# Other order and banks for the turned input norm and second norm, the last block of the down product in halves, and the arena's stationary tiles moved onto the weights' grid of 4096 bytes

## The chip, the cores and the metric

The kernel runs on one core of one Trainium2 chip. The metric is the device time of one execution in microseconds (us), lower is better. Engines: PE (TensorE), ACT (ScalarE), DVE (VectorE), POOL (GpSimd) and SP (SyncE, which here only issues the DMAs of the weights).

## What is computed

Two transformer blocks on 256 tokens of width 2048, all in float32. Cut to what matters here:

```python
def first_block(x, mem, ...):
    mem_h = rms_norm(mem, mem_norm_g)
    x = x + hybrid_mixer(rms_norm(x, mix_norm_g), w_in, ...)            # pooling and gated delta net
    x = x + memory_cross_attention(rms_norm(x, xa_norm_g), mem_h, w_xq, w_xkv, w_xo)
    x = x + conv_glu_ffn(rms_norm(x, ffn_norm_g), w_gate, w_up, ..., w_down)
    return rms_norm(x, final_norm_g)

def second_block(x, c, w_ada, b_ada, pre_norm_mix, ...):
    mod = silu(c) @ w_ada + b_ada
    shift_m, scale_m, gate_m, shift_f, scale_f, gate_f = split(mod, 6)
    h = rms_norm(x, pre_norm_mix) * (1 + scale_m) + shift_m
    o = concat(nsa_mixer(h @ w_in ...), moba_mixer(h @ w_in ...)) @ w_o
    x = x + gate_m * rms_norm(o, post_norm_mix)
    h = rms_norm(x, pre_norm_ffn) * (1 + scale_f) + shift_f
    f = square(relu(h @ w_up)) @ w_down
    return x + gate_f * rms_norm(f, post_norm_ffn)
```

## The kernel before, in words

**Products.** Every large product runs through `product` (PE), `phase`/`split_hi` (ACT) and `phase`/`split_lo` (DVE), one phase after another in the order of `plan()`: `wi0` to `wi4` (the first `w_in`), `mix_out`, `xkva`, `xkvb`, `xq`, `xo`, `ffn1a`, `down1a`, `ffn1b`, `down1b`, `w_in2a` to `w_in2c`, `w_oa`, `w_ob`, and four times `up2`, `down2`. A weight unit is 512 rows by 512 columns (428 in `wi`, 432 in `w_in2a`), a DMA by SP into one of four `raw` buffers. ACT rounds it to a high part `whi` (line 1295), DVE subtracts for the low part `wlo` (line 1715), in two halves each; the ring holds four halves, that is two units. SP, ACT and DVE are ahead of PE by at most these buffers: ACT waits for a half to be read (`mm_done`) before it overwrites it, SP for a unit to be split (`unit_used`). The first two units of a phase are split at the end of the phase ahead (`LEAD`).

Per unit PE makes 8 triples: high by high (line 869), low weights by high (870), high weights by low (871). The activations are the stationary operand (128 x 128; its load is the PEld row of the same line), the weights the moving one (up to 512 columns). The stationary tiles are turned (features on the partitions), split into a high and a low part too: `hhi`, `hlo` in fixed memory for most phases; in the arena, which is laid out anew for every stage, `mhi`, `mlo` (phases `xkva`, `xkvb`), `bhi`, `blo` (`ffn1a`, `ffn1b`), `flo` (`down1a`, `down1b`, whose high part `fhi` lies over `hhi` and `hlo`) and `f2hi`, `f2lo` (the four `down2`). In memory the ring begins at `ring0`, `hhi` 49152 bytes per partition further, the arena (`arena0`) 101920 bytes further. 24 of the iterations also carry the side product (`ada`): four more units per iteration, which DVE alone multiplies and adds (lines 1701 and 1703) for `mod`.

**A norm before a product.** The raw input is turned by PE (line 845, four transposes of 128 x 128 per group of two feature tiles, into one half of a two-bank tile), ACT takes the upper part out of the bank times the gain, DVE the lower part; the scale of the row is applied when the product is evacuated. For the input this is `raw_turn(0, k)`, `raw_upper(0, k)` (line 1356) and `raw_lower(0, k)` (line 1770) with k from 0 to 7, all in the two halves of `TA`; turn n waits for `norm_lo` n - 1. Turns 0 to 3 stand ahead of phase `wi0`, 4 and 5 after its first unit, 6 and 7 after its second. ACT and DVE take all eight before the third unit is split, and then compute `csig` (a sigmoid) on ACT and DVE.

**The second block's first norm** follows `down1b`. Its last addition to `x` (line 1784, 128 x 1024) and the product with the final gain (`final_gain`, line 2050) run on DVE after the first two units of `w_in2a` are split; ACT takes the squares (line 1587), DVE the mean, ACT the root (line 1596, for which it loads a table), DVE the reciprocal. `xn_f` is the scaled input: its first quarter by DVE (line 2066), the others by ACT (`pre2_scaled`, line 1601). `pre2_turn(g)` turns it into four banks, `pre2_full(g)` (DVE, line 2075) applies gain and shift, `hhi` is ACT's copy of that (line 1609), and `pre2_lower(g)` (DVE, line 2082) the rest. Groups 0 to 3 are turned ahead of `w_in2a`, 4 and 5 after its first unit, 6 and 7 after its second. DVE does all eight full and low parts before it goes on to the phase, where the first unit in its order is one of the side product, and the third weight unit comes after it.

## Time and profile before

| | |
|---|---|
| median of 3 runs | 3002.54 us (3001.13 to 3006.74) |
| profiled execution: its time, its span | 3002.88 us, 3001.1 us |
| mean granted PE clock | 0.971 |
| PE, PEld busy | 2847.8 us (95%), 2396.0 us (80%) |
| DVE, ACT, POOL busy | 1797.8 us (60%), 1309.7 us (44%), 182.4 us (6%) |
| HBM read | 575.66 MB, 193 GB/s over the span |
| chain that ended last | PE 90%, DVE 6%, ACT 2% |

Busy time of PE is modelled, since matmuls overlap: a matmul's duration is longer than the distance to the next one's start, and only gaps and distances between starts tell the pace. In a group of the profile, the numbers are count, busy time, mean ns of one, idle time of the engine before. In a timeline: start, duration, engine, line, operation, output and inputs, shape, how many were merged, and in brackets how long the engine had stood idle and what ended that. PEclk is the granted clock, 1.00 for the upper level (2.4 GHz) and 0.50 for the lower (1.2 GHz).

### The profile page before, as it was taken

What the parts mean: (1) busy time and instruction counts of PE and PEld (TensorE: products, weight loads), DVE (VectorE), ACT (ScalarE), POOL (GpSimd) and SP (SyncE); (2) the same over time, 40 slices, a digit from 0 to 9 for tenths busy, and PEclk for the clock granted to TensorE, in tenths of its full rate; (3) what the DMA queues carried; (4) which work ended last, traced back from release to release, by engine and by line L of the source; (5) the groups of instructions that cost most, each with busy time, mean ns of one, the idle gap of its engine ahead of it and who ended that gap; (6) DMA issues with size and microseconds to landing.
All of it is one profiled execution on the core that took longest, in us unless ns stands there. A gap on an engine that the chain in (4) does not pass through costs nothing.

```text
span 3001.1 us, 35854 instructions
## 1 busy us (share of the span) xinstructions
PE 2847.8 (95%) x13510; PEld 2396.0 (80%) x13510; DVE 1797.8 (60%) x2008; ACT 1309.7 (44%) x1620; POOL 182.4 (6%) x135
## 2 busy tenths in 40 slices
PE   8998989999899999999999889987879999999997
PEld 7998968888788888788888689776768787888885
DVE  4476567776466555665555477954675655744454
ACT  5454234454435445434444444324444444344442
POOL 0000520000000000000000004610000000000000
PEclk9999999999999999999999899978989999999998
DMA  7453038887556555675555388650455765755552
GB/s 261 155 170 110 1 142 278 272 269 259 181 197 224 182 182 182 228 246 179 174 187 199 124 302 298 226 182 15 157 179 176 245 227 207 267 192 186 183 184 96
DMA packets 292399, 579.57 MB, mean 193 GB/s; under 512 B 9072, under 2 KB 46096, under 8 KB 290992
## 3 DMA queue, kind: packets, MB, share of 16 engines
q1 hardware_dynamic: 290720, 565.03, 55.9%
q0 software_dynamic: 1552, 12.76, 1.1%
q8 instruction: 89, 1.46, 0.2%
q14 instruction: 38, 0.31, 0.0%
HBM read 575.66 MB, written 2.10 MB: 193 GB/s over the span
## 4 chain that ended last, share of the span: by engine, by line
PE 90%; DVE 6%; ACT 2%; issue 1%; DMA 0%; POOL 0%; DVEq 0%; SPq 0%; ACTq 0%
PE GP L869 27%; PE GP L870 26%; PE GP L871 26%; PE TA L845 2%; PE TB L468 2%; DVE ada_acc L1703 1%; PE TB L845 1%; DVE wlo L1715 1%; PE TA L1222 1%; PE GP L454 1%; PE TB L886 0%; DVE o L2148 0%; DVE x L2149 0%; ACT whi L1295 0%; DVE small L545 0%
## 5 line engine op out<-in xcount | busy, mean ns | idle before, releaser
L1715 DVE TENSOR_TENSOR wlo<-raw,whi 128x1024 fp32r<-128x1024 f32 (+2 forms) x904 | 1088.9, 1220 | 809.4 <-ACT whi L1295 799.2
L1295 ACT CAST whi<-raw 128x1024 fp32r<-128x1024 f32 (+2 forms) x904 | 921.3, 1029 | 1206.4 <-PE GP L871 1160.4
L869 PE MATMUL GP<-whi,hhi 128*128 128x512 f32 (+2 forms) x1792 | 695.8, 388 | 33.5 <-DVE wlo L1715 27.4
L870 PE MATMUL GP<-wlo,hhi 128*128 128x512 f32 (+2 forms) x1792 | 686.2, 383 | 0.0
L871 PE MATMUL GP<-whi,hlo 128*128 128x512 f32 (+2 forms) x1792 | 685.9, 383 | 0.0
L869 PEld LDWEIGHTS GP<-whi,hhi 128*128 128x128 f32 x1792 | 342.0, 191 | 88.7 <-issue 27.4
L871 PEld LDWEIGHTS GP<-whi,hlo 128*128 128x128 f32 x1792 | 341.4, 191 | 53.0
L870 PEld LDWEIGHTS GP<-wlo,hhi 128*128 128x128 f32 x1792 | 342.0, 191 | 51.8 <-issue 1.0
L1703 DVE SCALAR_TENSOR_TENSOR ada_acc<-raw,csig,ada_acc 128x512 f32<-128x512 f32 x360 | 284.4, 790 | 10.2
L869 PE MATMUL GP<-whi,bhi 128*128 128x512 f32 x704 | 280.4, 398 | 0.0
L870 PE MATMUL GP<-wlo,bhi 128*128 128x512 f32 x704 | 278.3, 395 | 0.0
L871 PE MATMUL GP<-whi,blo 128*128 128x512 f32 x704 | 278.2, 395 | 0.0
L869 PE MATMUL GP<-whi,f2hi 128*128 128x512 f32 x512 | 204.7, 400 | 4.7 <-DVE wlo L1715 4.7
L871 PE MATMUL GP<-whi,f2lo 128*128 128x512 f32 x512 | 202.5, 395 | 0.0
L870 PE MATMUL GP<-wlo,f2hi 128*128 128x512 f32 x512 | 202.4, 395 | 0.0
L871 PEld LDWEIGHTS GP<-whi,blo 128*128 128x128 f32 x704 | 132.3, 188 | 32.1
L870 PEld LDWEIGHTS GP<-wlo,bhi 128*128 128x128 f32 x704 | 132.3, 188 | 30.8
L869 PEld LDWEIGHTS GP<-whi,bhi 128*128 128x128 f32 x704 | 132.3, 188 | 30.8
L869 PE MATMUL GP<-whi,fhi 128*128 128x512 f32 x352 | 139.3, 396 | 2.5 <-DVE wlo L1715 2.5
L870 PE MATMUL GP<-wlo,fhi 128*128 128x512 f32 x352 | 140.7, 400 | 0.0
L871 PE MATMUL GP<-whi,flo 128*128 128x512 f32 x352 | 137.0, 389 | 0.0
L869 PEld LDWEIGHTS GP<-whi,f2hi 128*128 128x128 f32 x512 | 96.2, 188 | 29.1 <-issue 6.5
(394 smaller groups left out, 2688.2 us busy)
## 6 DMA issues: line engine op xcount, KB each, us to landing
raw<-in_w_up SPq DMA_DIRECT2D x108, 1024.0 KB, 5.4
raw<-in_w_down SPq DMA_DIRECT2D x108, 1024.0 KB, 5.0
raw<-in_w_ada SPq DMA_DIRECT2D x96, 1024.0 KB, 5.1
raw<-in_w_gate SPq DMA_DIRECT2D x44, 1024.0 KB, 5.1
raw<-in_w_in SPq DMA_DIRECT2D x48, 856.0 KB, 4.7
raw<-in_w_xkv SPq DMA_DIRECT2D x32, 1024.0 KB, 5.5
raw<-in_w_in SPq DMA_DIRECT2D x24, 1024.0 KB, 5.0
raw<-in_w_in SPq DMA_DIRECT2D x24, 864.0 KB, 5.0
```

Source lines behind the costliest of these rows:

```text
L454: m = pe.matmul(o[:, h * T:h * T + u["L"]], l, r, start=(d == 0), stop=(d == n - 1), skip_group_check=True)
L468: m = pe.matmul(bank[:, j * P:j * P + P], l, r, start=(d == 0), stop=(d == len(terms) - 1), skip_group_check=True)
L845: return pe.transpose(dst, src, ident[0:n, 0:n] if n != P else ident)
L869: pe.matmul(o, ahi[:, kt, t], whi[r][:, k, 0:q.width], start=first, stop=False)
L870: pe.matmul(o, ahi[:, kt, t], wlo[r][:, k, 0:q.width], start=False, stop=False)
L871: m = pe.matmul(o, alo[:, kt, t], whi[r][:, k, 0:q.width], start=False, stop=last)
L1222: m = pe.matmul(TA[:, 512:543], w1c[:, l, :], rc1[:, l, :], start=(l == 0), stop=(l == 31))
L1295: nc.scalar.copy(whi[(2 * g + s) % NRING][:, :, 0:q.width], raw[j % NSLOT][:, 2 * s:2 * s + 2, 0:q.width])\
L1703: m = nc.vector.scalar_tensor_tensor(ada_acc[:, :], raw[j % NSLOT][:, k, :], c, ada_acc[:, :], ALU.mult, ALU.add)
L1715: TTo(wlo[r][:, :, 0:q.width], raw[j % NSLOT][:, 2 * s:2 * s + 2, 0:q.width], whi[r][:, :, 0:q.width].bitcast(F32), ALU.subtract).then_inc ...
```

## The change

Four things:

1. `level()` rounds an arena address up to the next one with the remainder that `ring0` has by 4096. It is applied ahead of `mhi`/`mlo`, of `bhi`/`blo` (and so `flo` and the tiles behind them) and of `f2hi`/`f2lo`: each moves up by 480 bytes.
2. The input's norm: turns 2 and 3, 6 and 7 go to `TB`; turns 4 to 7 follow `wi0`'s first unit; ACT and DVE take banks 6 and 7 after the third unit's split; the squares come one unit later, the sigmoid for `csig` four units later, and DVE's product for it behind `wi4`.
3. The last block of `down1b` is added and multiplied by the final gain row half by row half (`last_block`), ACT squares each half as it comes, and a square root of a constant ahead of the squares loads the root's table.
4. The second norm: six groups are turned ahead of `w_in2a`, into six banks (`GP` 2 and the second half of `TB` are new), 6 and 7 after its first unit; DVE goes two full parts, two low parts; groups 6 and 7 come after the third unit's split on ACT and DVE.

```diff
--- before.py
+++ after.py
+        def level(at):
+            return at + (ring0 - at) % 4096
...
-        ar = Arena(); ar.at = arena0 + 4 * NH * 2 * D
+        ar = Arena(); ar.at = level(arena0 + 4 * NH * 2 * D)
         mhi = ar("mhi", [P, KT, T], F32R); mlo = ar("mlo", [P, KT, T], F32R)
...
-        ar = Arena()
+        ar = Arena(); ar.at = level(arena0)
         bhi = ar("bhi", [P, KT, T], F32R); blo = ar("blo", [P, KT, T], F32R)
         fhi = nc.alloc_sbuf_tensor_at("fhi", [P, 24, T], F32R, offset=hh0); flo = ar("flo", [P, 24, T], F32R)
...
         o3 = ar("o3", [P, NH, D])
+        ar.at = level(ar.at)
         f2hi = ar("f2hi", [P, 16, T], F32R); f2lo = ar("f2lo", [P, 16, T], F32R)
...
-        pre2_bank = [TA[:, 0:512], TA[:, 512:1024], TB[:, 0:512], GP[:, 3, :]]
-
-        def raw_bank(n):
-            return TA[:, 512 * (n % 2):512 * (n % 2) + 512]
+        pre2_bank = [TA[:, 0:512], TA[:, 512:1024], TB[:, 0:512], GP[:, 3, :], GP[:, 2, :], TB[:, 512:1024], TA[:, 0:512], TA[:, 512:1024]]
+
+        def raw_bank(n, s=None):
+            t = TB if s == 0 and n % 4 >= 2 else TA
+            return t[:, 512 * (n % 2):512 * (n % 2) + 512]
...
-                if n >= 2:
+                if s == 0:
+                    if k >= 4:
+                        pe.wait_ge(S("norm_lo"), k - 3)
+                else:
                     pe.wait_ge(S("norm_lo"), n - 1)
...
-                    points={(0, 0, u): lambda u=u: (raw_turn(0, 2 * u + 4), raw_turn(0, 2 * u + 5)) for u in range(2)})
+                    points={(0, 0, 0): lambda: [raw_turn(0, k) for k in range(4, 8)]})
...
             def pre2_turn(g):
-                pe.wait_ge(*((S("p2_x"), g // 2) if g >= 2 else (S("p2_x0"), 1)))
+                pe.wait_ge(*((S("p2_x"), g // 2) if g >= 2 else (S("p2_x0"), 4)))
                 if g == 3:
                     pe.wait_ge(S("evac1"), 1 + PH["down1b"].ev1)
-                if g >= 4:
-                    pe.wait_ge(S("norm_f"), g - 3)
+                if g == 5:
+                    pe.wait_ge(S("ada_read"), PH["w_in2a"].ada0 + 1)
+                if g >= 6:
+                    pe.wait_ge(S("norm_lo"), 32 + g - 5)
                 for j in range(2):
                     for h in range(NH):
-                        m = turn(pre2_bank[g % 4][:, j * T + h * P:j * T + h * P + P], xn_f[:, h, (2 * g + j) * P:(2 * g + j + 1) * P])
+                        m = turn(pre2_bank[g][:, j * T + h * P:j * T + h * P + P], xn_f[:, h, (2 * g + j) * P:(2 * g + j + 1) * P])
                 m.then_inc(S("norm_t"), 1)
 
-            for g in range(4):
+            for g in range(6):
                 pre2_turn(g)
             product(PH["w_in2a"], hhi, hlo, lambda u: (S("norm_lo"), 32 + 2 * u + 2), first=lambda: None,
-                    points={(0, 0, u): lambda u=u: (pre2_turn(2 * u + 4), pre2_turn(2 * u + 5)) for u in range(2)})
+                    points={(0, 0, 0): lambda: (pre2_turn(6), pre2_turn(7))})
...
             split_hi(order[0], 0, 1)
-            for k in range(4, 8):
-                raw_upper(0, k)
-            nc.scalar.activation(csig[:, :], cvec[:, :], ACT.Sigmoid).then_inc(S("csig"), 1)
+            raw_upper(0, 4)
+            raw_upper(0, 5)
...
-                  head={3: [lambda it: raw_square(0, (0,))], 4: [lambda it: raw_square(0, (1,))], 5: [lambda it: raw_root(0)]})
+                  head={3: [lambda it: (raw_upper(0, 6), raw_upper(0, 7))], 4: [lambda it: raw_square(0, (0,))], 5: [lambda it: (raw_square(0, (1,)), raw_root(0))],
+                        7: [lambda it: nc.scalar.activation(csig[:, :], cvec[:, :], ACT.Sigmoid).then_inc(S("csig"), 1)]})
...
-                act.wait_ge(*((S("fin_g"), b + 1) if i else (S(f"evac{b % 2}"), 2 + PH["down1b"].ev0 + b // 2)))
+                if b < 3:
+                    act.wait_ge(*((S("fin_g"), b + 1) if i else (S(f"evac{b % 2}"), 2 + PH["down1b"].ev0 + b // 2)))
                 for h in range(NH):
+                    if b == 3:
+                        act.wait_ge(*((S("p2_x0"), h + 2) if i else (S("evac1"), 1 + PH["down1b"].ev1) if h else (S("p2_x0"), 1)))
...
+            nc.scalar.activation(froot[:, 0:1], C("ones", 0, 1), ACT.Sqrt)
             final_squares(3, 0)
             final_squares(3, 1)
...
-            pre2_scaled(1)
-            for g in range(8):
-                if g in (2, 4):
-                    pre2_scaled(g // 2 + 1)
+            def pre2_upper(g):
                 act.wait_ge(S("norm_f"), g + 1)
                 nc.scalar.copy(hhi[:, 2 * g:2 * g + 2, :], fbx[g % 2].rearrange("p (a b) -> p a b", b=T)).then_inc(S("norm_hi"), 1)
-            phase(PH["w_in2a"], store(PH["w_in2a"], p2, lastcol=NSA_W - W2A), head={5: [lambda it: act.wait_ge(S("fin_x"), 2)]})
+
+            pre2_scaled(1)
+            pre2_scaled(2)
+            for g in range(6):
+                if g == 4:
+                    pre2_scaled(3)
+                pre2_upper(g)
+            phase(PH["w_in2a"], store(PH["w_in2a"], p2, lastcol=NSA_W - W2A), head={3: [lambda it: (pre2_upper(6), pre2_upper(7))],
+                                                                                         5: [lambda it: act.wait_ge(S("fin_x"), 2)]})
...
-            phase(PH["wi0"], {}, head={4: [lambda it: raw_mean(0)], 5: [lambda it: raw_scale(0)]})
+            phase(PH["wi0"], {}, head={3: [lambda it: (raw_lower(0, 6), raw_lower(0, 7))], 5: [lambda it: (raw_mean(0), raw_scale(0))]})
             for k in range(1, 5):
                 phase(PH[f"wi{k}"], slots(todo, f"wi{k}"), ahead=(k < 4))
+            dve.wait_ge(S("csig"), 1)
+            link(TTo(csig[:, :], csig[:, :], cvec[:, :], ALU.mult))
             dve.wait_ge(S("cst_in"), 16)
...
+            def last_block(it):
+                dve.wait_ge(S("mm_done"), block_end(PH["down1b"], it, 3) + NRING)
+                c = slice(1536, 2048)
+                TTo(x[:, 0, c], GP[:, 2, :], x[:, 0, c], ALU.add).then_inc(S("p2_x0"), 1)
+                TTo(x[:, 1, c], GP[:, 3, :], x[:, 1, c], ALU.add).then_inc(S("evac1"), 1)
+                dve.wait_ge(S("p2_x0"), 1)
+                TTo(xg[:, 0, c], x[:, 0, c], fgb[:, c], ALU.mult).then_inc(S("p2_x0"), 1)
+                dve.wait_ge(S("evac1"), 1 + PH["down1b"].ev1)
+                TTo(xg[:, 1, c], x[:, 1, c], fgb[:, c], ALU.mult).then_inc(S("p2_x0"), 1)
+
+            for b in range(3):
                 hooks[5 * b + 7] = hooks[5 * b + 7] + [lambda it, b=b: final_gain(b)]
+            hooks[22] = [last_block]
...
-            pre2_full(0)
-            for g in range(1, 8):
+            def pre2_pair(g):
                 pre2_full(g)
-                pre2_lower(g - 1)
-            pre2_lower(7)
+                pre2_full(g + 1)
+                pre2_lower(g)
+                pre2_lower(g + 1)
+
+            for g in (0, 2, 4):
+                pre2_pair(g)
 
             def final_x(h):
                 nc.vector.tensor_scalar(x[:, h, :], xg[:, h, :], frs[:, h:h + 1], None, ALU.mult).then_inc(S("fin_x"), 1)
 
-            phase(PH["w_in2a"], {}, head={3: [lambda it: final_x(0)], 4: [lambda it: final_x(1)]})
+            phase(PH["w_in2a"], {}, head={3: [lambda it: pre2_pair(6)], 4: [lambda it: final_x(0)], 5: [lambda it: final_x(1)]})
```

The instructions on ACT at the start. Names: `whi0` to `whi3` are the ring's high halves, `raw2` holds the third unit. Before:

```order
L1295 CAST whi2_51<-raw1 128x2x428
L1295 CAST whi3_52<-raw1 128x2x428
L1356 ACTIVATE hhi<-TA,tab 128x256 x8
L1410 ACT_TABLE_LOAD
L1410 ACTIVATE csig<-tab 128x16
L1295 CAST whi0_49<-raw2 128x2x428
```

and with the change:

```order
L1307 CAST whi2_51<-raw1 128x2x428
L1307 CAST whi3_52<-raw1 128x2x428
L1368 ACTIVATE hhi<-TA,tab 128x256 x4
L1307 CAST whi0_49<-raw2 128x2x428
L1307 CAST whi1_50<-raw2 128x2x428
L1368 ACTIVATE hhi<-TB,tab 128x256 x4
```

The third unit moved ahead of two of the four banks, the table load and the sigmoid.

DVE in the second norm, from group 5's full part (two instructions per group at line 2075 before, 2107 now) to the third unit. Before:

```order
L2075 TENSOR_SCALAR flat<-TA,tab,shifts 128x256 x2
L2082 TENSOR_TENSOR hlo<-flat,hhi 128x512
L2075 TENSOR_SCALAR flat<-TB,tab,shifts 128x256 x2
L2082 TENSOR_TENSOR hlo<-flat,hhi 128x512
L2075 TENSOR_SCALAR flat<-GP,tab,shifts 128x256 x2
L2082 TENSOR_TENSOR hlo<-flat,hhi 128x512 x2
L1701 TENSOR_SCALAR ada_acc<-raw2,csig 128x512
L1703 SCALAR_TENSOR_TENSOR ada_acc<-raw2,csig,ada_acc 128x512 x3
L1715 TENSOR_TENSOR wlo0_53<-raw3,whi0_49 128x2x432
```

and with the change:

```order
L2107 TENSOR_SCALAR flat<-TB,tab,shifts 128x256 x2
L2114 TENSOR_TENSOR hlo<-flat,hhi 128x512 x2
L1722 TENSOR_SCALAR ada_acc<-raw2,csig 128x512
L1724 SCALAR_TENSOR_TENSOR ada_acc<-raw2,csig,ada_acc 128x512 x3
L1736 TENSOR_TENSOR wlo0_53<-raw3,whi0_49 128x2x432
L1736 TENSOR_TENSOR wlo1_54<-raw3,whi1_50 128x2x432
L2107 TENSOR_SCALAR flat<-TA,tab,shifts 128x256 x4
L2114 TENSOR_TENSOR hlo<-flat,hhi 128x512 x2
```

The side product's unit and the third unit now stand ahead of groups 6 and 7.

## Rows read from the trace of the kernel before

**Rows 1.** The page of the kernel before, part 1: busy time of each engine.

```profile
PE 2847.8 (95%) x13510; PEld 2396.0 (80%) x13510; DVE 1797.8 (60%) x2008; ACT 1309.7 (44%) x1620; POOL 182.4 (6%) x135
```

**Rows 2.** Groups of instructions by shape, PE: count, busy us, mean ns of one.

```profile
L870 PE MATMUL GP<-wlo,hhi 128*128 128x512 f32 x1216 | 477.1, 392 | 0.0
L870 PE MATMUL GP<-wlo,bhi 128*128 128x512 f32 x704 | 278.3, 395 | 0.0
L870 PE MATMUL GP<-wlo,f2hi 128*128 128x512 f32 x512 | 202.4, 395 | 0.0
L870 PE MATMUL GP<-wlo,fhi 128*128 128x512 f32 x352 | 140.7, 400 | 0.0
L871 PE MATMUL GP<-whi,flo 128*128 128x512 f32 x352 | 137.0, 389 | 0.0
L870 PE MATMUL GP<-wlo,mhi 128*128 128x512 f32 x256 | 101.2, 395 | 0.0
```

**Rows 3.** Timeline of PE in `w_oa`, `hhi` stationary: the 1st and 18th `L870`.

```profile
2150.25 0.39 PE L870 MATMUL GP<-wlo,hhi 128*128 128x512 f32 x1
...
2161.81 0.39 PE L870 MATMUL GP<-wlo,hhi 128*128 128x512 f32 x1
```

**Rows 4.** Timeline of PE in `ffn1a`, `bhi` stationary: the 1st and 17th `L870`.

```profile
1000.27 0.40 PE L870 MATMUL GP<-wlo,bhi 128*128 128x512 f32 x1
...
1011.47 0.40 PE L870 MATMUL GP<-wlo,bhi 128*128 128x512 f32 x1
```

**Rows 5.** Timeline of PE in `down1a`, `fhi` stationary: the 1st and 18th `L870`.

```profile
1310.04 0.40 PE L870 MATMUL GP<-wlo,fhi 128*128 128x512 f32 x1
...
1321.94 0.40 PE L870 MATMUL GP<-wlo,fhi 128*128 128x512 f32 x1
```

**Rows 6.** Timeline just after a sum of the side product: 1st and 4th `L870`.

```profile
1841.23 0.39 PE L870 MATMUL GP<-wlo,hhi 128*128 128x512 f32 x1
...
1843.31 0.39 PE L870 MATMUL GP<-wlo,hhi 128*128 128x512 f32 x1
```

**Rows 7.** Timeline of the start: ACT, DVE, PE; idle before in brackets.

```profile
24.74 1.57 ACT L1356 ACTIVATE hhi<-TA,tab 128x256 fp32r<-128x256 f32 x4 [4.02 <-PE TA L845]
...
28.73 2.01 DVE L1715 TENSOR_TENSOR wlo<-raw,whi 128x856 fp32r<-128x856 f32 x2 [0.69 <-ACT whi L1295]
...
29.93 0.70 PE L869 MATMUL GP<-whi,hhi 128*128 128x428 f32 x1 [4.79 <-DVE wlo L1715]
```

**Rows 8.** Windows: busy of PE, PEld, DVE, ACT, POOL, then PEclk, DMA share, GB/s.

```profile
30.00:35.00 5.00, 5.00 (x19) 4.72 (x20) 2.86 (x4) 5.00 (x7) 0.00 (x0) 0.70 0.57 179
```

**Rows 9.** The same view around the second norm.

```profile
1733.00:1736.00 3.00, 2.84 (x8) 2.66 (x9) 3.00 (x4) 0.00 (x0) 0.00 (x0) 0.50 0.80 302
1736.00:1744.00 8.00, 8.00 (x42) 7.54 (x40) 6.21 (x9) 1.74 (x2) 0.00 (x0) 0.98 1.01 387
```

**Rows 10.** Timeline of the second norm, all engines.

```profile
1697.36 1.22 DVE L1784 TENSOR_TENSOR x<-GP,x 128x1024 f32<-128x1024 f32 x1
...
1701.68 1.28 ACT L1596 ACT_TABLE_LOAD   x1
...
1704.36 1.97 PE L845 MATMUL TA<-cst,xn_f 128*128 128x128 f32 x8 [8.95 <-DVE xn_f L2066]
...
1709.81 0.70 PE L869 MATMUL GP<-whi,hhi 128*128 128x432 f32 x1 [1.78 <-issue]
...
1719.63 0.46 PE L869 MATMUL GP<-whi,hhi 128*128 128x432 f32 x1 [1.26 <-DVE hlo L2082]
...
1729.08 0.48 DVE L1701 TENSOR_SCALAR ada_acc<-raw,csig 128x512 f32<-128x512 f32 x1
...
1731.95 2.03 DVE L1715 TENSOR_TENSOR wlo<-raw,whi 128x864 fp32r<-128x864 f32 x2
...
1733.16 0.70 PE L869 MATMUL GP<-whi,hhi 128*128 128x432 f32 x1 [7.67 <-DVE wlo L1715]
...
1741.99 1.74 ACT L1295 CAST whi<-raw 128x864 fp32r<-128x864 f32 x2 [10.30 <-DMA raw<-in_w_in]
```

More of the change, by code:

```diff
@@ L162, in program @@
         hh0 = (nc.sbuf_base + 31) // 32 * 32
+        assert (hh0 - ring0) % 4096 == 0
         hhi = fixed("hhi", [P, KT, T], F32R)
@@ L926, in raw_turn @@
                     for h in range(NH):
-                        m = turn(raw_bank(n)[:, j * T + h * P:j * T + h * P + P], X[:, h, (2 * k + j) * P:(2 * k + j + 1) * P])
+                        m = turn(raw_bank(n, s)[:, j * T + h * P:j * T + h * P + P], X[:, h, (2 * k + j) * P:(2 * k + j + 1) * P])
                 m.then_inc(S("norm_t"), 1)
@@ L1355, in raw_upper @@
                 for j in range(2):
-                    m = nc.scalar.activation(hi[:, 2 * k + j, :], raw_bank(n)[:, j * T:j * T + T], ACT.Copy, scale=gains[:, g_, 2 * k + j:2 * k + j + 1])
+                    m = nc.scalar.activation(hi[:, 2 * k + j, :], raw_bank(n, s)[:, j * T:j * T + T], ACT.Copy, scale=gains[:, g_, 2 * k + j:2 * k + j + 1])
                 m.then_inc(S("norm_hi"), 1)
@@ L1769, in raw_lower @@
                 for j in range(2):
-                    m = nc.vector.scalar_tensor_tensor(lo[:, 2 * k + j, :], raw_bank(n)[:, j * T:j * T + T], gains[:, g_, 2 * k + j:2 * k + j + 1],
+                    m = nc.vector.scalar_tensor_tensor(lo[:, 2 * k + j, :], raw_bank(n, s)[:, j * T:j * T + T], gains[:, g_, 2 * k + j:2 * k + j + 1],
                                                        hi[:, 2 * k + j, :].bitcast(F32), ALU.mult, ALU.subtract)
@@ L1835, in _ @@
             split_lo(order[0], 0, 1)
-            for k in range(4, 8):
-                raw_lower(0, k)
-            dve.wait_ge(S("csig"), 1)
-            link(TTo(csig[:, :], csig[:, :], cvec[:, :], ALU.mult))
+            raw_lower(0, 4)
+            raw_lower(0, 5)
             def gate_first():
@@ L2052, in _ @@
             hooks = add_to_x(PH["down1b"])
-            for b in range(4):
+            def last_block(it):
[8 more added lines that the diff above has]
+            for b in range(3):
                 hooks[5 * b + 7] = hooks[5 * b + 7] + [lambda it, b=b: final_gain(b)]
+            hooks[22] = [last_block]
             hooks[4] = [lambda it: modulation(0, 0, 4)]
@@ L2074, in pre2_full @@
                     kt = 2 * g + j
-                    m = nc.vector.tensor_scalar(fbx[g % 2][:, j * T:j * T + T], pre2_bank[g % 4][:, j * T:j * T + T], gains[:, 4, kt:kt + 1],
+                    m = nc.vector.tensor_scalar(fbx[g % 2][:, j * T:j * T + T], pre2_bank[g][:, j * T:j * T + T], gains[:, 4, kt:kt + 1],
                                                 shifts[:, 0, kt:kt + 1], ALU.mult, ALU.add)
```

## The prediction

> **What bounds the kernel now.** I read the page first: PE is busy 95% of the span and no other engine over 60% [rows 1]. So only two kinds of change can move the time: one in the pace at which PE takes its matmuls, and one in the gaps in which PE stands still. The sum is made against the profiled execution (3002.88 us, with 1.8 us outside its span of 3001.1); the median of the runs is 3002.54, 0.3 us under it.
>
> For the pace I took the groups by shape. All large products are the same triple (`L869`, `L870`, `L871`), 512 columns wide, with different stationary tiles. With `hhi`/`hlo` as stationaries a matmul takes 392 ns in the mean, with the arena's `bhi`, `f2hi` and `mhi` 395, and where `fhi` and `flo` are mixed, 400 and 389 [rows 2]. These are latencies, and what counts is the distance between starts. In the timeline, 17 triples on `hhi` take 2161.81 - 2150.25 = 11.56 us, 680 ns each [rows 3]; 16 on `bhi`/`blo` take 11.20 us, 700 ns each [rows 4]; 17 on `fhi`/`flo` take 11.90 us, again 700 [rows 5]. It isn't the work beside them: `w_oa` and `down1a` both run with the side product, `ffn1a` runs without it. What the slower ones share is that a stationary lies in the arena.
>
> For the gaps I took the timelines of the two places that the change rearranges. At the start, PE stands 4.79 us before the third weight unit: DVE makes its low half at 28.73, after the norm's last two banks, whose upper parts ACT takes from 24.74 on [rows 7]. After the gap the granted clock falls to its lower level (1.2 GHz): the 5 us window has 0.70, that is 3.0 us at 0.50 [rows 8]. At the second norm, PE stands 8.95, 1.78, 1.26 and 7.67 us [rows 10], and again the clock is 0.50 after the last gap [rows 9].
>
> **The change, part 1: the arena's stationaries.** `ring0` to `arena0` is 101920 bytes by the tiles' shapes, 24 x 4096 + 3616. Every arena tile of a product so lies 3616 past the weights' grid of 4096, `hhi` and `hlo` lie 0 past it (49152 = 12 x 4096), and the change puts the former to 0 too, by 480 bytes. It adds no instruction. Triples with an arena stationary: `ffn1a` and `ffn1b` 384 + 320 = 704, the four `down2` 512, `down1a` and `down1b` 192 + 160 = 352, `xkva` and `xkvb` 256, as the counts in [rows 2] say; 1824 in all. If they go from 700 to 680 ns: 1824 x 20 ns = 36.5 us. Not all of it, since `hhi` triples don't always run at 680: after an interruption of the stream (turns, or the sum of the side product) the first three take 2.08 us, 693 ns each [rows 6]. Some 54 such interruptions lie in the arena's phases (22 gate and up turns, 8 + 4 single ones, 10 sums, 10 starts); 54 x 3 x 13 ns = 2.1 us. I take **34 us**. The bounds are 0 (place doesn't matter) and 36.5. For a loss see the rivals.
>
> All of it lies on PE's path: ACT and DVE wait for PE in these phases, not the other way, as 60% and 44% of busy time allow [rows 1]. What could be late next is the weights' transfer. With the side product, 8 + 4 units of 1.05 MB go with 64 triples: 12.6 MB in 64 x 0.68 + 1 = 44.5 us, 283 GB/s, under the 387 that one window shows [rows 9]. DVE then has 16 x 1.24 + 4 x 3.1 = 32 us of work in 44.5. Neither becomes the bound.
>
> The row speaks against a rule here. By the Trainium skill, page "TensorE: Matmul & The Clock Gate", Part 2, step 1, loading the next stationary takes no SBUF bandwidth from the running matmul, and by its section on the back-to-back gap 512 columns are 216 ns apart whatever the tiles. By that, part 1 would be worth 0 and all triples would take 647 ns; the trace disagrees with both (680 and 700).
>
> **Part 2: the start.** Turns 0 to 3 go to four banks (two of `TA`, two of `TB`), 4 to 7 all follow the first unit, and on ACT and DVE the third unit's split stands ahead of banks 6 and 7. Step by step: turns 4 and 5 end at about 19.3 as before, 6 and 7 at 20.4 (the input's last columns must have landed; POOL, which waits for them all, went on at 18.4, a bound of a microsecond on this). The second unit then runs 20.4 to 25.0. ACT takes banks 4 and 5 until 20.7 and the third unit until 22.5, DVE its low half until 23.7: before 25.0, so PE goes on. Banks 6 and 7 follow on ACT until 24.1 and on DVE until 25.5, due at 29.7 for the fourth unit. The gap of 4.79 us goes, and with it 3.0 us at half clock, in which PE did the work of 1.6: 1.4 us more. **6.2 us**, between 4 and 6.5. The squares and the root come one unit later and are due only at the first evacuation; the sigmoid with its table load (1.28 us, as [rows 10] show one) moves behind that evacuation, where ACT waits for PE. `csig`'s product now stands on DVE ahead of the delta net, 0.2 us, covered by the turn that DVE waits for there.
>
> **Part 3: the second norm.** From PE's last matmul of `down1b` (1704.36 - 8.95 = 1695.41) to the fifth unit of `w_in2a` (its split starts at 1741.99, its first matmul 2.2 us later, 1744.2) it is now 48.8 us. In order:
> - *The wait.* The last block's addition (1.22 us) is halved, so ACT's four squares start some 0.55 us earlier, and the square root's table load (1.28 us) is over before them. The root waited for the load's end, about 0.5 us after the mean was there. 8.95 becomes about 7.95.
> - *The turns.* Eight transposes take 1.97 us at half clock [rows 10]; six groups of four so take 5.2. DVE's order (two full, two low) has the second low part about 4.4 us after the first turn starts, so PE doesn't wait the 1.78 us any more. Before: 3.7 + 1.8 = 5.5.
> - *The first unit.* 1709.81 to 1717.14, 7.3 us, most of it at half clock. Same work after about the same idle time; I take 7.3 again, between 5 and 8.6 (24 matmuls at 0.36).
> - *Second unit.* Two groups, then no wait for a low part: 1.0 + 4.7. Before 2.5 + 4.6 with the 1.26 us.
> - *Turns and the long wait.* 1.2 + 7.67 us go. DVE has the low part of group 5 some 10.9 us after the first turn, then the side product's unit (from 1729.08 to the split at 1731.95: 2.9), then the third unit's (2.0): 15.9 us after the first turn, when PE is 5.2 + 7.3 + 1.0 + 4.7 = 18.2 past it. Covered by 2.3 us.
> - *Third and fourth unit.* 9.4 at full clock, before 11.05, since the stretch after the gap ran at 0.50.
>
> Sum: 7.95 + 5.2 + 7.3 + 5.7 + 9.4 = 35.6 against 48.8: **13.2 us**, between 8 and 15. What is queued behind the moved work: the scaling of `x` (2 x 1.28 us) now follows the pair 6, 7 on DVE, and the fifth unit's low half ends up about 0.6 us ahead of PE. That is the tightest spot. Raw units: the fifth is asked for when the side product's unit is free, now about 14 us earlier; before, it came late (ACT waited 10.3 us until 1741.99) as POOL's loads for the compression ran at the same time. These now start behind it, since POOL still waits for the last low part.
>
> **Sum.** 34 + 6.2 + 13.2 = 53.4; 3002.9 - 53.4 = 2949.5, against the median 2949. Anything within 0.2% (6 us) would be no change that can be told.
>
> **Rivals.**
> - *A. The place is not the reason.* Another thing that all arena tiles share sets the pace (that they lie above `hhi`, say), and the triples stay at 700. For it: no tile of a product lies low and off the grid, so the trace can't tell the two apart. Against it: the loads of `flo` and `fhi`, which differ in both, also differ in time (400 and 389). Then only parts 2 and 3 count: 3002.9 - 19.4 = 2983.5. The rule of the Trainium skill's page "TensorE: Matmul & The Clock Gate" cited above gives this time too.
> - *B. The norms' new order makes new waits.* Full parts in pairs hold ACT up, and the fifth unit comes late or the sixth (ACT waits for both scalings of `x`): half of part 3 and some of part 2 go, 2949 + 9 = 2958; the placement is untouched.
> - *C. Slower.* In the one place where loads on and off the grid alternate, the matmul under `flo`'s load takes 400 ns. If sharing the weights' remainder makes tiles this high collide, every arena matmul takes 400 instead of 395: 3 x 1824 x 5 ns = 27 us lost, less 19.4 gained: 3010.8. It decides from 3.5 ns a matmul on. Against it: `hhi` shares the remainder and has the shortest distance.
>
> **How the numbers follow.** The forecast has 0.75 (its own range 2942 to 2957), A 0.13, B 0.07, C 0.03, 0.02 for the rest near no change. The time is the forecast's, 2949. The range must take in B and reach to A: 2941 to 2985. Chances: faster 0.95 (forecast, A, B), same 0.02, slower 0.03.
>
> **What would show it.** Right: `L870` on `bhi`, `f2hi`, `mhi` at 392 or less in the groups and 680 ns between starts in `ffn1a`; no wait of PE for `wlo` within the first 60 us and a clock of 1.00 from 20 to 40; at the second norm one wait of about 8 us and none of over 1 us before the third unit. Part 1 is wrong if the distance stays 700. Part 3 is wrong if PE waits for `wlo` or `hlo` between the first turn and the sixth unit. If the sum is far under 53 with all three steps as said, a later phase has become bound by DVE or the transfers, and ACT would show long waits for `raw`.

## The result, and the profile after

| | before | after |
|---|---|---|
| median of four runs | 3002.26 us | 2951.80 us |
| range of the runs | 3001.13 to 3006.74 | 2948.91 to 2956.72 |
| profiled execution, its span | 3002.88, 3001.1 | 2952.63, 2950.9 |
| PE busy | 2847.8 us | 2812.7 us |

The ratio is 0.9831, with a 95% interval from 0.9814 to 0.9848: 50.5 us less. The forecast was 2949.0, with a range from 2941 to 2985.

The page of the changed kernel, busy time and granted clock, against [rows 1]:

```profile
PE 2812.7 (95%) x13510; PEld 2393.9 (81%) x13510; DVE 1794.3 (61%) x2010; ACT 1308.7 (44%) x1620; POOL 183.5 (6%) x135
...
PEclk9998999999999999999999999978989999999998
```

PE has the same number of instructions and 35 us less of busy time, and the rest of the 50 us went from its idle time. By shape, the groups that answer to [rows 2] (columns: line, engine, tiles, shape, count, busy us, mean ns of one, idle before):

```profile
L877 PE MATMUL GP<-wlo,hhi 128*128 128x512 f32 x1216 | 476.8, 392 | 0.0
...
L877 PE MATMUL GP<-wlo,bhi 128*128 128x512 f32 x704 | 273.9, 389 | 0.0
...
L877 PE MATMUL GP<-wlo,f2hi 128*128 128x512 f32 x512 | 199.8, 390 | 0.0
...
L877 PE MATMUL GP<-wlo,fhi 128*128 128x512 f32 x352 | 137.7, 391 | 0.0
L878 PE MATMUL GP<-whi,flo 128*128 128x512 f32 x352 | 137.6, 391 | 0.0
L877 PE MATMUL GP<-wlo,mhi 128*128 128x512 f32 x256 | 99.7, 389 | 0.0
```

With `bhi`, `f2hi` and `mhi` a matmul fell by 5 to 6 ns, the pair of 400 and 389 became 391 twice, and `hhi` stayed at 392. In the timeline of `ffn1a`, 16 triples now take 10.89 us, 681 ns each, where [rows 4] had 11.20:

```profile
934.52 0.40 PE L877 MATMUL GP<-wlo,bhi 128*128 128x512 f32 x1
...
945.41 0.39 PE L877 MATMUL GP<-wlo,bhi 128*128 128x512 f32 x1
```

The start, timeline of ACT, DVE and PE, which answers to [rows 7]:

```profile
18.92 1.04 PE L852 MATMUL TB<-cst,x 128*128 128x128 f32 x8
...
19.72 0.44 PE L876 MATMUL GP<-whi,hhi 128*128 128x428 f32 x1
...
20.13 1.73 ACT L1307 CAST whi<-raw 128x856 fp32r<-128x856 f32 x2
21.14 2.00 DVE L1736 TENSOR_TENSOR wlo<-raw,whi 128x856 fp32r<-128x856 f32 x2
21.73 1.59 ACT L1368 ACTIVATE hhi<-TB,tab 128x256 fp32r<-128x256 f32 x4
```

The third unit's low half (`L1736`) is made at 21.1, not at 28.7, ahead of the last two banks. The 4.79 us gap is gone, and with it the lower clock: the window that had 0.70 in [rows 8] has 1.00 (columns: window, its length, busy PE, PEld, DVE, ACT, POOL with counts, clock, DMA share, GB/s).

```profile
25.00:30.00 5.00, 5.00 (x28) 4.83 (x27) 2.74 (x3) 3.91 (x5) 0.00 (x0) 1.00 1.04 372
30.00:35.00 5.00, 5.00 (x27) 4.84 (x26) 1.82 (x4) 4.97 (x7) 0.00 (x0) 1.00 0.79 254
```

The second norm, PE's timeline, against [rows 10]. The turns follow one another, the first unit begins right behind them, and the waits of 1.78, 1.26 and 7.67 us are gone. What is left is one wait of 8.06 and, in the stretch shown, two small ones on `wlo`:

```profile
1676.13 1.97 PE L852 MATMUL TA<-cst,xn_f 128*128 128x128 f32 x8 [8.06 <-DVE xn_f L2098]
...
1680.80 0.44 PE L876 MATMUL GP<-whi,hhi 128*128 128x432 f32 x1
...
1685.59 1.03 PE L852 MATMUL TA<-cst,xn_f 128*128 128x128 f32 x8
1686.38 0.44 PE L876 MATMUL GP<-whi,hhi 128*128 128x432 f32 x1
...
1696.29 0.43 PE L876 MATMUL GP<-whi,hhi 128*128 128x432 f32 x1 [0.26 <-DVE wlo L1736]
...
1702.56 0.43 PE L876 MATMUL GP<-whi,hhi 128*128 128x432 f32 x1 [1.34 <-DVE wlo L1736]
```

To see where the 50.2 us of the span came from I laid the two traces side by side by the products' phases, each from its first matmul to its last:

| stretch | before | after | less |
|---|---|---|---|
| first four units of `wi0` | 28.96 | 21.85 | 7.1 |
| `mhi` (`xkva`, `xkvb`) | 185.18 | 180.58 | 4.6 |
| `bhi` (`ffn1a`, `ffn1b`) | 279.05 + 231.64 | 271.92 + 225.68 | 13.1 |
| `fhi` (`down1a`, `down1b`) | 138.65 + 112.62 | 136.65 + 109.50 | 5.1 |
| `f2hi` (four `down2`) | 93.72 + 93.72 + 90.23 + 94.06 | 91.41 + 93.01 + 87.71 + 91.84 | 7.8 |
| last matmul of `down1b` to last of `w_in2a` | 144.89 | 131.05 | 13.8 |
| everything else | | | -1.3 |

The first row is part 2 of the change, the sixth parts 3 and 4 (the prediction takes them together as its part 3), the four between them part 1 (30.6 us). The negative rest is mostly in `mix_out`, a product that the change leaves alone: it took 1.15 us longer, because the granted clock was lower for more of it (see below).

### The profile page after: what moved, and what is told of

It reads as the page before. It is cut to its first block, busy times and chain, and to the rows that moved or that the text cites. A ratio compares the mean times of both kernels' runs of the same rounds, so it can differ in the third digit from the quotient of the medians.

```text
span 2950.9 us, 35855 instructions
## 1 busy us (share of the span) xinstructions
PE 2812.7 (95%) x13510; PEld 2393.9 (81%) x13510; DVE 1794.3 (61%) x2010; ACT 1308.7 (44%) x1620; POOL 183.5 (6%) x135
## 4 chain that ended last, share of the span: by engine, by line
PE 90%; DVE 6%; ACT 2%; issue 1%; DMA 1%; POOL 0%; DVEq 0%; SPq 0%; ACTq 0%
PE GP L876 26%; PE GP L878 26%; PE GP L877 26%; PE TA L852 2%; PE TB L474 2%; DVE ada_acc L1724 1%; PE TB L852 1%; DVE wlo L1736 1%; PE TA L1234 1%; PE GP L460 1%; PE TB L893 1%; ACT whi L1307 0%; DVE o L2183 0%; DVE x L2184 0%; DVE small L551 0%
## 5 line engine op out<-in xcount | busy, mean ns | idle before, releaser
L1736 DVE TENSOR_TENSOR wlo<-raw,whi 128x1024 fp32r<-128x1024 f32 (+2 forms) x904 | 1086.2, 1219 | 779.5 <-ACT whi L1307 769.1
```

The costliest lines, as they stand in the source:

```text
L1736: TTo(wlo[r][:, :, 0:q.width], raw[j % NSLOT][:, 2 * s:2 * s + 2, 0:q.width], whi[r][:, :, 0:q.width].bitcast(F32), ALU.subtract).then_inc ...
```

## The experiments

Twelve kernels ran. They ask three things: whether place and order act apart from each other, what about the place matters, and which piece of each new order carries its gain. In short diffs, `-` is the changed kernel and `+` the experiment, unless said otherwise.

### Each half of the change alone: `e1_place`, `e2_norms`

`e1_place`, against the kernel before:

```diff
+        def level(at):
+            return at + (ring0 - at) % 4096
...
-        ar = Arena(); ar.at = arena0 + 4 * NH * 2 * D
+        ar = Arena(); ar.at = level(arena0 + 4 * NH * 2 * D)
...
-        ar = Arena()
+        ar = Arena(); ar.at = level(arena0)
         bhi = ar("bhi", [P, KT, T], F32R); blo = ar("blo", [P, KT, T], F32R)
...
+        ar.at = level(ar.at)
         f2hi = ar("f2hi", [P, 16, T], F32R); f2lo = ar("f2lo", [P, 16, T], F32R)
```

> The kernel before with the arena's stationaries at the weights' remainder and nothing else. Placement theory (part 1 as predicted): triples of mhi, bhi, fhi/flo and f2hi go from about 700 to about 681 ns, 34 us less, 2968 us. Interruption theory (rival A: the difference in before came from what ran beside those products, not from the address): triples stay at 700 ns, 3002 us. What the trace of the change suggests in between: the triples fall, but a little of it is given back in half-clock stretches, about 31 us less, 2971.

Measured: 2972.12 us, ratio 0.9897 [0.9882, 0.9912], 30.4 us less. The groups of its trace:

```profile
L874 PE MATMUL GP<-wlo,bhi 128*128 128x512 f32 x704 | 273.9, 389 | 0.0
...
L874 PE MATMUL GP<-wlo,f2hi 128*128 128x512 f32 x512 | 200.0, 391 | 0.0
```

They are those of the changed kernel to 1 ns, so the interruption theory falls. Most of the 3.6 us between 34 and 30.4 is a matter of the clock, shown below.

`e2_norms`, against the changed kernel:

```diff
         def level(at):
-            return at + (ring0 - at) % 4096
+            return at
```

> The change without its placement: only the order and the banks of the two norms, and the halves of the last block. If the two parts are independent, parts 2 and 3 as predicted give 19.4 us less than before, 2983 us; by the trace of the change (7.2 and 13.8 us) 21 less, 2981. If the norms' gain needed the faster products (its weights arriving in time), it would be under 12 us, over 2990.

Measured: 2982.81 us, ratio 0.9936 [0.9922, 0.9949], 19.7 us less than before. Its arena triples stay at 700 ns, and its `f2hi` phases are as long as before to 0.01 us each. The two halves add up within what the intervals allow (some 4 us on each): 30.4 + 19.7 = 50.1, and the whole change gave 50.5. The norms' order doesn't lean on the faster products.

### What about the address: `e3_grid`, `e4_low`, `e5_grid2`, `e12_grid3`

All arena tiles of a product lay off the weights' grid before and lie on it now, so the change alone can't say which grid it is. One kernel can hold several remainders, since each tile has its own phases. `e3_grid`:

```diff
-        ar = Arena(); ar.at = level(arena0 + 4 * NH * 2 * D)
+        ar = Arena(); ar.at = level(arena0 + 4 * NH * 2 * D) + 64
...
-        ar = Arena(); ar.at = level(arena0)
+        ar = Arena(); ar.at = level(arena0) + 256
...
-        fhi = nc.alloc_sbuf_tensor_at("fhi", [P, 24, T], F32R, offset=hh0); flo = ar("flo", [P, 24, T], F32R)
+        fhi = nc.alloc_sbuf_tensor_at("fhi", [P, 24, T], F32R, offset=hh0); ar.at += 256; flo = ar("flo", [P, 24, T], F32R)
...
-        ar.at = level(ar.at)
+        ar.at = level(ar.at) + 1024
```

> The change with four different remainders against the weights: mhi and mlo 64 bytes on, bhi and blo 256, flo 512, f2hi and f2lo 1024. Theory 64 (a stationary is slow only where its address is not a multiple of 64 bytes): every triple stays at 681 ns, 2952 us. Theory 4096 (it must lie at the weights' own remainder, as the change puts it): all four kinds go back to 700 ns, some 34 us more, 2985. A border in between (128, 512 or 1024) shows as some kinds fast and some slow.

Measured: 2955.69 us, ratio 0.9843 [0.9825, 0.9861]. `bhi` and `blo` now lie 256 bytes past the grid, `flo` 512 (256 and 256 more), `f2hi` and `f2lo` 1024. Only `mhi`, 64 bytes past it, is slow again; 256, 512 and 1024 are as good as 0:

```profile
L877 PE MATMUL GP<-wlo,bhi 128*128 128x512 f32 x704 | 273.9, 389 | 0.0
L877 PE MATMUL GP<-wlo,f2hi 128*128 128x512 f32 x512 | 199.8, 390 | 0.0
L878 PE MATMUL GP<-whi,flo 128*128 128x512 f32 x352 | 137.7, 391 | 0.0
...
L877 PE MATMUL GP<-wlo,mhi 128*128 128x512 f32 x256 | 101.2, 395 | 0.0
```

Neither theory holds as it was put: 64 isn't enough, and 4096 isn't needed.

`e4_low`, a pad of 32 bytes ahead of `hhi`:

```diff
+        fixed("shim", [P, 8])
         hh0 = (nc.sbuf_base + 31) // 32 * 32
-        assert (hh0 - ring0) % 4096 == 0
```

> The change with a pad of 32 bytes ahead of hhi, so that hhi, hlo and fhi, which lay at the weights' remainder in both kernels, lie 32 bytes off it; the arena's stationaries stay on it. Address theory: the triples of hhi (1216) and of fhi (352) go to 700 ns, 1568 x 19 ns = 30 us more, 2982. Region theory (the lower part of the memory is fast, the arena fast for another reason): hhi's stay at 681 ns, 2952 us.

Measured: 2979.33 us, ratio 0.9922 [0.9904, 0.994], 27.5 over the change. Low tiles and arena have changed places:

```profile
L877 PE MATMUL GP<-wlo,hhi 128*128 128x512 f32 x1216 | 484.1, 398 | 0.0
...
L877 PE MATMUL GP<-wlo,bhi 128*128 128x512 f32 x704 | 274.0, 389 | 0.0
```

`hhi`'s triples are 700 ns apart (1150 of them in the timeline), `bhi`'s 681. So the region is not the reason, the address is. One group did not follow: the triples of `wi0` to `wi4`, 428 columns wide, lose nothing here, 32 bytes off the grid. `wi4` (64 triples) takes 39.57 us from its first matmul to its last, and 39.81 in the change, with the same stationary tiles.

`e5_grid2` has other remainders in the same four places (`mhi` 128, `bhi` 64, `flo` 128, `f2hi` 384), `e12_grid3` three more (`mhi` 96, `bhi`, `blo` and `flo` 160, `f2hi` 224).

> The change with other remainders against the weights: mhi and mlo 128 bytes on, bhi and blo 64, flo 128, f2hi and f2lo 384. In the run before this one 64 was slow (mhi) and 256, 512 and 1024 fast. Theory 128: mhi, fhi/flo and f2hi at 681 ns, bhi (704 triples) at 700, 13 us more than the change, 2965. Theory 256: mhi, fhi/flo, f2hi and bhi all at 700 ns, 34 us more, 2985. If only mhi was slow there for a reason of its own, bhi stays at 681 too and mhi does not.

> The change with mhi and mlo 96 bytes off the weights' remainder, bhi, blo and flo 160, f2hi and f2lo 224. Period theory (a stationary is fast only where its distance from the weights is a multiple of 256 bytes, as 0, 256, 512 and 1024 were and 32, 64, 128, 192 and 384 were not): all three at 700 ns, 34 us over the change, 2985. If it is a matter of nearness or of certain remainders, one of them is at 681 or below.

Measured: `e5_grid2` 2979.75 us, ratio 0.9926 [0.9904, 0.9949]; `e12_grid3` 2984.32, ratio 0.9941 [0.9922, 0.9959]. The groups of `e5_grid2`:

```profile
L877 PE MATMUL GP<-wlo,bhi 128*128 128x512 f32 x704 | 277.4, 394 | 0.0
...
L877 PE MATMUL GP<-wlo,f2hi 128*128 128x512 f32 x512 | 202.0, 395 | 0.0
...
L877 PE MATMUL GP<-wlo,mhi 128*128 128x512 f32 x256 | 101.0, 395 | 0.0
```

All are slow: 128 is no grid either, and 384 is 128 past a multiple of 256. So `bhi` (160), `f2hi` (224) and `mhi` (96) in `e12_grid3`:

```profile
L877 PE MATMUL GP<-wlo,bhi 128*128 128x512 f32 x704 | 277.6, 394 | 0.0
L877 PE MATMUL GP<-wlo,f2hi 128*128 128x512 f32 x512 | 202.2, 395 | 0.0
...
L877 PE MATMUL GP<-wlo,mhi 128*128 128x512 f32 x256 | 101.5, 396 | 0.0
```

### Absolute or against the weights: `e6_all64`, `e7_ring64`, `e8_all128`

A pad ahead of the ring moves weights and stationaries together (`[P, 16]` is 64 bytes, `[P, 32]` in `e8_all128` 128):

```diff
+        fixed("shim", [P, 16])
         ring0 = (nc.sbuf_base + 31) // 32 * 32
```

`e7_ring64` has the same pad and a second one, also of 64 bytes, ahead of `hh0`, and `level` counts from `hh0`. The stationaries are back on multiples of 128 bytes, the weights alone lie 64 off them, and every stationary lies 64 bytes past the weights' remainder.

> The change with a pad of 64 bytes ahead of the weights' ring: weights and all stationaries still have one and the same remainder, but each address lies 64 bytes off a multiple of 128. Relative theory (stationaries and weights must agree, the words of the change): all triples 681 ns, 2952 us. Absolute theory (a stationary must lie on a multiple of 128 bytes): all 3040 triples of 512 columns at 700 ns, 58 us more, 3010.

> The change with the weights' ring alone 64 bytes off a multiple of 128, stationaries all on one. Relative theory: all triples 700 ns, 3010 us. Absolute theory for the stationary alone: 681 ns, 2952 us. If the moving side has the same rule, the triples are slower than 681, by an amount that no row shows yet.

> The change with a pad of 128 bytes ahead of the weights' ring: weights and stationaries then lie on multiples of 256 bytes (in the change, 128 off). By the theory that 128 is all that counts, 681 ns and 2952 us. If 256 were worth something over 128, all triples fall below 681, and the time below 2949.

Measured: `e6_all64` 2950.57 us, ratio 0.9828 [0.9799, 0.9857]; `e7_ring64` 3008.09, ratio 1.0019 [1.0008, 1.003]; `e8_all128` 2949.95, ratio 0.9826 [0.9797, 0.9854]. The groups of `e6_all64`, then of `e7_ring64`:

```profile
L878 PE MATMUL GP<-wlo,hhi 128*128 128x512 f32 x1216 | 477.0, 392 | 0.0
...
L878 PE MATMUL GP<-wlo,bhi 128*128 128x512 f32 x704 | 274.0, 389 | 0.0
```

```profile
L878 PE MATMUL GP<-wlo,hhi 128*128 128x512 f32 x1216 | 483.6, 398 | 0.0
...
L878 PE MATMUL GP<-wlo,bhi 128*128 128x512 f32 x704 | 278.0, 395 | 0.0
```

This decides it. Where all addresses lie 64 bytes off together nothing is lost; where only the distance between weights and stationaries is wrong, all 3040 triples take 700 ns, and a kernel that has both new norm orders is 5.7 us slower than the one before. Together with the other runs, the distance (stationary less weights, modulo 256) has been tried at seven of the eight multiples of 32: 0 is fast (as 0, 256, 512 and 1024 bytes), and 32 (before, `e4_low`), 64 (`e3_grid`, `e5_grid2`, `e7_ring64`), 96, 128, 160 and 224 are slow. 192 was not tried: the expectation of `e12_grid3` counts it for `e7_ring64`, where the distance is 64.

### What carries the norms' gain: `e9_undo1`, `e10_undo2`, `e11_finx`

The start and the second norm lie 1400 us apart, so one kernel can undo a piece of each. `e9_undo1` takes back the whole start, and in the second norm the halves:

```diff
-            t = TB if s == 0 and n % 4 >= 2 else TA
+            t = TA
...
-                    points={(0, 0, 0): lambda: [raw_turn(0, k) for k in range(4, 8)]})
+                    points={(0, 0, u): lambda u=u: (raw_turn(0, 2 * u + 4), raw_turn(0, 2 * u + 5)) for u in range(2)})
...
-            raw_upper(0, 4)
-            raw_upper(0, 5)
+            for k in range(4, 8):
+                raw_upper(0, k)
...
-            for b in range(3):
+            for b in range(4):
                 hooks[5 * b + 7] = hooks[5 * b + 7] + [lambda it, b=b: final_gain(b)]
-            hooks[22] = [last_block]
```

> The change with two places set back that lie 1400 us apart, each read from its own stretch of the trace: the start's order and banks as before, and the last block of down1b in one piece as before (the table of the root is still loaded early). Start: the first product ends 7.2 us later than in the change if the order there is the whole gain. Last block: the stretch from down1b's last matmul to w_in2a's first, 13.1 us in the change and 14.8 before, becomes 13.8 to 14.2 if the halves are worth about as much as the early table, 13.1 if the halves are worth nothing. Sum: 8 us over the change, 2960.

Measured: 2957.34 us, ratio 0.9847 [0.9832, 0.9863]. The first product is 6.9 us longer than in the change, and the old wait is back:

```profile
30.24 0.70 PE L876 MATMUL GP<-whi,hhi 128*128 128x428 f32 x1 [4.79 <-DVE wlo L1731]
...
1681.10 1.97 PE L852 MATMUL TA<-cst,xn_f 128*128 128x128 f32 x8 [8.48 <-DVE xn_f L2092]
```

The wait ahead of the turns is 8.48 instead of 8.06, so the halves are worth 0.4 us there, less than the 0.7 to 1.1 I had expected. In the stretch from `down1b`'s last matmul to `w_in2a`'s first (13.42 us instead of 13.12) it can't be seen: kernels with the halves and the new order have 13.0 to 13.5 there.

`e10_undo2` keeps halves and early table and takes back the second norm's order, banks and pairs, and puts the sigmoid back into the start:

```diff
-            for g in range(6):
+            for g in range(4):
                 pre2_turn(g)
...
-            for g in (0, 2, 4):
-                pre2_pair(g)
+            pre2_full(0)
+            for g in range(1, 8):
+                pre2_full(g)
+                pre2_lower(g - 1)
+            pre2_lower(7)
...
             raw_upper(0, 5)
+            nc.scalar.activation(csig[:, :], cvec[:, :], ACT.Sigmoid).then_inc(S("csig"), 1)
```

> The change with two other places set back: the order, the banks and the pairs of the second norm as before (its halves and its early table kept), and the sigmoid of the condition and its product back in the middle of the start. Second norm: by the prediction the order and the banks carry it, w_in2a ends 12 to 13 us later than in the change, with the half clock, the waits on wlo and the long wait of before all back. If what counted was that x was there a microsecond earlier, it ends at most 4 us later. Sigmoid: under 0.5 us if the first units' weights are ahead of TensorE, 1.5 to 3 us if its table loads on ScalarE stand in the way of the second unit. Sum 13 us over the change, 2965.

Measured: 2961.86 us, ratio 0.9868 [0.9853, 0.9883]. PE's timeline at the second norm:

```profile
1670.08 1.97 PE L852 MATMUL TA<-cst,xn_f 128*128 128x128 f32 x8 [8.07 <-DVE xn_f L2094]
...
1675.53 0.43 PE L876 MATMUL GP<-whi,hhi 128*128 128x432 f32 x1 [1.78 <-issue]
...
1682.62 0.47 PE L876 MATMUL GP<-whi,hhi 128*128 128x432 f32 x1 [1.25 <-DVE hlo L2110]
...
1696.14 0.70 PE L876 MATMUL GP<-whi,hhi 128*128 128x432 f32 x1 [7.67 <-DVE wlo L1732]
```

The last three waits of [rows 10] are back, to 0.01 us. From `down1b`'s last matmul to `w_in2a`'s last it takes 142.16 us against 131.05 in the change: the order carries 11.1 of the 13.8. The first product (`wi0` to `wi4`) is no longer than in the change, 250.8 against 251.3, and the traces with the new start have 249.8 to 252.1, so nothing can be seen of the sigmoid's place. The long wait brings the lower clock back, but the first unit runs at the full clock here (0.43 for its first matmul, 0.70 in [rows 10]), with the old order.

`e11_finx` moves `x`'s writing back by one and two units, and ACT's wait for it behind the split:

```diff
-            phase(PH["w_in2a"], store(PH["w_in2a"], p2, lastcol=NSA_W - W2A), head={3: [lambda it: (pre2_upper(6), pre2_upper(7))],
-                                                                                         5: [lambda it: act.wait_ge(S("fin_x"), 2)]})
+            hooks = store(PH["w_in2a"], p2, lastcol=NSA_W - W2A)
+            hooks[6] = [lambda it: act.wait_ge(S("fin_x"), 2) if isinstance(it, int) and it == 0 else None] + hooks[6]
+            phase(PH["w_in2a"], hooks, head={3: [lambda it: (pre2_upper(6), pre2_upper(7))]})
...
-            phase(PH["w_in2a"], {}, head={3: [lambda it: pre2_pair(6)], 4: [lambda it: final_x(0)], 5: [lambda it: final_x(1)]})
+            phase(PH["w_in2a"], {}, head={3: [lambda it: pre2_pair(6)], 5: [lambda it: final_x(0)], 6: [lambda it: final_x(1)]})
```

> The change with the writing back of x in w_in2a's first columns moved one and two units later on VectorE, and ScalarE's wait for it put behind the split of the unit ahead of the store. In the change ScalarE waits 7.1 us there and TensorE 1.8 us in three waits on wlo. If that wait causes them, they go and the time falls by up to 1.8 us, 2950.0, below what the runs can tell; if VectorE's side product (3.1 us each) causes them, they stay, and x's two halves only move them.

Measured: 2949.24 us, ratio 0.9831 [0.9818, 0.9845], the change's own ratio. The waits of ACT and PE between 1670 and 1800, first of the changed kernel (ACT), then of this one (PE and ACT; columns: who waited, for what, us in total, times, longest):

```profile
ACT whi L1307 <- DVE x L2126: 7.1, 1, 7.1
```

```profile
PE GP L876 <- DVE wlo L1737: 2.4, 3, 2.1
...
ACT p L1386 <- DVE x L2127: 4.4, 1, 4.4
```

ACT's wait shrank from 7.1 to 4.4 and no longer stands ahead of a split, yet PE waits 2.4 us on `wlo` where it waited 1.8. ACT's wait was not the reason. What PE waits for is DVE's queue. In the change DVE works without a gap between 1689.7 and 1704.6, and ahead of the fifth unit's low half it scales half of `x` (from 1697.02, 1.28 us) and makes the side product (from 1698.22, 3.10 us). With the scaling one unit later, PE's wait at the fifth unit went from 1.34 to 0.16 us, and one of 2.07 came at the seventh: the wait moved. What it is worth to move the side product, I have not tested. I know of no version here that beats the change.

## Why the prediction was right, and where its terms were off

**What bounds the kernel.** PE's pace and PE's gaps, as read from [rows 1]: all 50 us came from these two, 35 from PE's busy time and 15 from its idle time. The forecast saved 53.4 us and the change saved 50.5: part 1 gave 3.6 us less than forecast and the other two 1.5 more, so part of the nearness of the total is luck.

**Part 1: forecast 34 us, measured 30.4 alone.** The count (1824 triples) and the pace held: in the timelines the triples that follow one another go from 700 to 681 ns. That the address is the reason held too, by `e1_place` and `e4_low`; that the grid is one of 4096 bytes did not, since 256 is enough (`e3_grid`). 1824 x 19 ns = 34.7 us. Measured in the change, of what 19 ns a triple would give by product: `mhi` 4.6 of 4.9, `bhi` 13.1 of 13.4, `fhi` 5.1 of 6.7, `f2hi` 7.8 of 9.7. Most of what is missing, 3.4 of 4.1 us, is in two phases, `down1a` (2.0 of 3.6) and the second `down2` (0.7 of 2.4), and both times it is the clock. PE waits about 2.5 us for a low half there, before and after. Before, the granted clock stayed at 1.00 behind this wait. In `e1_place` it fell to its lower level of 1.2 GHz in `down1a` for nine matmuls, which are 427 ns apart instead of about 230, 1.6 us in all:

```profile
1225.57 0.47 PE L869 MATMUL GP<-whi,fhi 128*128 128x512 f32 x1 [2.52 <-DVE wlo L1715]
```

```profile
1215.39 0.53 PE L873 MATMUL GP<-whi,fhi 128*128 128x512 f32 x1 [2.66 <-DVE wlo L1719]
1215.71 0.63 PE L874 MATMUL GP<-wlo,fhi 128*128 128x512 f32 x1
```

The part of the sum that was off is "All of it lies on PE's path": the gain lies there, but I had not priced that shorter phases move each short wait in time, and that the clock's answer to the same wait can change. It is not the new pace that does it. `e2_norms`, with the old pace, had the fall in `down1a` too (2.52 us of wait, seven matmuls, 1.5 us), and not in the second `down2`. `e10_undo2` and `e8_all128`, with the new pace, did not have it in `down1a`. In `e10_undo2` PE waits 2.62 us there, until 1204.71, the matmuls behind it keep their 0.39 to 0.40 us, and the phase takes 135.08 us against 136.65 in the change. So which kernel pays these 1.6 us is luck as far as the runs go. What decides it for a wait of 2.5 us, no run here shows. It is seen elsewhere too: in `mix_out`, whose work and addresses the change leaves alone, seven matmuls ran at the lower clock before and 13 after, and the phase went from 101.83 to 102.98 us.

**Part 2: forecast 6.2 us, measured 7.1 (6.9 by `e9_undo1`).** The gap and the lower clock went as said. (3.0 us at half clock hold the work of 1.5 us and not of 1.6, so the forecast should have read 6.3.) Most of the difference is the second unit: I let it start at 20.4, since the input's last columns bound the turns; they had landed, the turns came at 18.05 and 18.92, and it started at 19.72. The rest can't be told: the traces with the new start have 21.2 to 22.4 us for the first four units, so 7.1 is good to about half a us. That the sigmoid is covered held.

**Part 3: forecast 13.2 us, measured 13.8.** This is to the end of `w_in2a`. To its fifth unit, where the forecast was made, it is 14.3: 34.5 us instead of 48.8, and 0.5 us were lost behind it. The sum is right to about 1 us, its terms less so. From the end of `down1b`'s last matmul:

| term | forecast | measured |
|---|---|---|
| wait for the first turn | 7.95 | 8.06 |
| six turns | 5.2 | 4.67 |
| first unit | 7.3 | 4.79 |
| two turns, second unit | 5.7 | 5.58 |
| third and fourth unit, to the fifth | 9.4 | 11.39 |
| sum | 35.6 | 34.49 |

Two errors stand against each other, so that the sum came out so near is luck. The first unit: I took half clock for most of it, as in [rows 10], but the clock had risen by 1680.8. `e10_undo2` shows that this is no merit of the order, since its first unit ran at the full clock under the old one. `e1_place` shows it too: it has the old order, 9 slow matmuls in its first unit where before had 16, and takes 143.87 us over the stretch instead of 144.89. About 1 us of the 13.8, then, is the clock's and not the change's. The fourth and the fifth unit: I had the fifth's low half 0.6 us ahead of PE and called it the tightest spot. It was the right spot with the wrong sign: PE waited 1.34 us there and 0.26 one unit earlier. By the prediction's own test (no wait of PE for `wlo` between the first turn and the sixth unit) part 3 failed in this step, by 1.6 us; its other signs held, and so did those of parts 1 and 2. ACT's wait for `x`, part of rival B, did appear, 7.1 us long, but by `e11_finx` PE's waits don't hang on it. They hang on what DVE does in between, one of the scalings of `x` included.

Of the first term, the wait, 8.95 became 8.48 with the table loaded early and 8.06 with the halves as well: 0.9 together, where I had 1.0.

**The rivals.** A (the place is not the reason) falls by `e1_place` and `e4_low`; the latter is the case that A's "for" said the trace lacked, a tile that lies low and off the grid, and it is slow. B happened in small (the 1.6 us of part 3). C, the slower end, had the collision the wrong way round: sharing the remainder is the fast case. What it priced, arena matmuls that go from 395 to 400 ns, came in no run: `bhi`, `f2hi` and `mhi` have 394 to 397 at a wrong distance, 395 before. `e7_ring64` is 5.7 us slower than before for another reason: its `hhi` triples are slow too, 1216 x 19 ns = 23 us, more than the norms give back.

**The rule that I weighed.** By the Trainium skill, page "TensorE: Matmul & The Clock Gate", Part 2, step 1, the load of a stationary takes no bandwidth from the running matmul. The page says nothing of addresses; that the place would be worth 0 was what I took to follow from it, and the runs disagree with that: moving nothing but addresses, the same instructions go from 681 to 700 ns a triple and back. That load and moving rows meet at the same place in the memory when their distance is not a multiple of 256 bytes would fit all the runs, but it is an explanation only; no run looks at the memory itself.

## What to carry to other kernels

Where every matmul brings its own stationary and the moving side is 512 columns wide, give stationaries and moving tiles the same remainder modulo 256 bytes within a partition; it costs no instruction and was worth 19 ns in 700 for each three matmuls. Look for it by grouping the same instruction by its operands, in distances between starts: equal work with two paces on two tiles is worth an address check before anything else. In a norm between two products, spend banks so that the turns follow one another, and let DVE's next weight half stand ahead of the norm parts that are due later. And don't count on a forecast to a microsecond where short waits of TensorE are about: the granted clock behind one of 2.5 us came out either way here.
